# Where the 24 conditioning slabs of a two-layer diffusion trunk are loaded and multiplied: all ahead of layer 0, or 4 + 6 + 14

## What is computed

```
def trunk_layer(x, cvec, l, ...):
    mod = silu(cvec) @ w_mod[l] + b_mod[l]         # (6, 1024) per group: shift, scale, gate, shift, scale, gate
    h = rmsnorm(x, g[0]) * (1 + mod[1]) + mod[0]   # needs mod 0 and 1
    m = token_mixers(h)                            # 18 column panels of w_in, retention, attention, HGRN2, w_br, w_o
    x = x + mod[2] * rmsnorm(m, g[1])
    h = rmsnorm(x, g[2]) * (1 + mod[4]) + mod[3]
    f = swiglu(h) if l == 0 else moe(h)            # dense feed-forward in layer 0, top 2 of 8 experts in layer 1
    x = x + mod[5] * rmsnorm(f, g[3])
```

## Time and profile before

| | before |
|---|---|
| time, median of 3 runs (lowest, highest) | 1983.29 us (1982.0, 1985.23) |
| the profiled execution: its time | 1984.04 us |
| the profiled execution: span, first to last instruction | 1982.1 us |
| busy PE, DVE, ACT, POOL in the span | 88%, 63%, 50%, 6% |
| mean granted clock of TensorE | 0.936 of full speed |
| start of panel 0 of layer 0, from the span's start | 142.9 us |
| dense feed-forward on PE | 486 to 683 us |

### The profile page before, as it was taken

How to read it: one execution, slowest core, us unless ns; L and a number is a source line. 1 busy time by engine, 2 the same in 40 slices (tenths; PEclk the granted TensorE clock), 3 DMA queues, 4 the chain that set the end, 5 groups by cost and what they waited for, 6 DMA issues and landing times.

```text
span 1982.1 us, 21106 instructions
## 1 busy us (share of the span) xinstructions
PE 1750.0 (88%) x8190; PEld 1399.3 (71%) x8191; DVE 1257.7 (63%) x1081; ACT 988.9 (50%) x930; POOL 126.1 (6%) x78
## 2 busy tenths in 40 slices
PE   4569999976999779999875999989898989898996
PEld 1128888865788668888765777878787878787773
DVE  1115579843544365598643887878686868686872
ACT  3114353333444264543332767767676767675751
POOL 1001013200000010033100000000000000000000
PEclk9869999987999879999985999999999999998998
DMA  9994544414443424534232879798797979797850
GB/s 400 427 401 170 185 164 150 164 60 192 169 190 150 158 86 175 196 134 165 96 136 100 313 288 361 287 362 337 313 368 275 378 271 372 281 368 272 349 206 22
DMA packets 55795, 470.22 MB, mean 237 GB/s; under 512 B 6352, under 2 KB 6400, under 8 KB 8496
## 3 DMA queue, kind: packets, MB, share of 16 engines
q1 hardware_dynamic: 52848, 458.25, 59.8%
q0 software_dynamic: 2880, 11.02, 1.4%
HBM read 465.05 MB, written 4.19 MB: 237 GB/s over the span
## 4 chain that ended last, share of the span: by engine, by line
PE 83%; DMA 6%; ACT 4%; DVE 4%; issue 3%; POOL 0%; SPq 0%; POOLq 0%; ACTq 0%; DVEq 0%
PE ps L927 24%; PE ps L928 24%; PE ps L929 24%; DMA ring<-in_w_mod 5%; ACT w_hi L711 2%; PE ps L1097 2%; PE ps L989 1%; PE ps L1321 1%; PE ps L1059 1%; PE ps L901 1%; DVE ring_lo L1618 1%; PE ps L969 1%; PE ps L921 1%; DMA ring<-in_w_in 1%; ACT ring_lo L700 0%
## 5 line engine op out<-in xcount | busy, mean ns | idle before, releaser
L1618 DVE TENSOR_TENSOR ring_lo<-ring,w_hi 128x2048 fp32r<-128x2048 f32 x297 | 680.0, 2292 | 232.1 <-ACT w_hi L711 232.0
L927 PE MATMUL ps<-ring_lo,h_hi 128*128 128x512 f32 x1520 | 611.0, 402 | 31.0 <-issue 25.1
L711 ACT ACTIVATE w_hi<-ring 128x2048 fp32r<-128x2048 f32 x297 | 568.0, 1913 | 106.8 <-PE ps L929 97.3
L927 PEld LDWEIGHTS ps<-ring_lo,h_hi 128*128 128x128 f32 x1520 | 289.8, 191 | 93.9 <-issue 33.9
L929 PE MATMUL ps<-w_hi,h_hi 128*128 128x512 f32 x880 | 346.2, 393 | 0.0
L928 PE MATMUL ps<-w_hi,h_lo 128*128 128x512 f32 x880 | 346.1, 393 | 0.0
L1557 DVE TENSOR_TENSOR ring_lo<-ring,ring_lo 128x2048 fp32r<-128x2048 f32 x76 | 182.6, 2405 | 236.4 <-ACT ring_lo L700 235.7
L700 ACT ACTIVATE ring_lo<-ring 128x2048 fp32r<-128x2048 f32 x92 | 176.1, 1916 | 260.9 <-PE ps L929 215.4
L929 PE MATMUL ps<-ring_lo,h_hi 128*128 128x512 f32 x640 | 252.2, 394 | 0.0
L928 PE MATMUL ps<-ring_lo,h_lo 128*128 128x512 f32 x640 | 252.0, 394 | 0.0
L927 PE MATMUL ps<-ring_lo,act_hi 128*128 128x512 f32 x440 | 181.9, 413 | 41.6 <-DVE ring_lo L1618 41.6
(11 more groups left out here) (266 smaller groups left out, 1474.4 us busy)
## 6 DMA issues: line engine op xcount, KB each, us to landing
ring<-in_w_ff SPq DMA_DIRECT2D x297, 1024.0 KB, 6.9
ring<-in_w_in SPq DMA_DIRECT2D x36, 2048.0 KB, 8.1
ring<-in_w_mod SPq DMA_DIRECT2D x24, 2048.0 KB, 12.4
ring<-in_w_br SPq DMA_DIRECT2D x6, 2048.0 KB, 7.9
ring<-in_w_o SPq DMA_DIRECT2D x4, 2048.0 KB, 7.7
out<-state_out POOLq DMA_DIRECT2D x4, 512.0 KB, 4.5
x_sb<-in_x POOLq DMA_DIRECT2D x1, 1024.0 KB, 28.8
state<-in_s_ret POOLq DMA_DIRECT2D x2, 512.0 KB, 25.6
```

The costliest lines, as they stand in the source:

```text
L711: A(w_hi[p], ring[i % SLOTS][:, p * UNIT:(p + 1) * UNIT], ACT.Copy).then_inc(hi_ready[p], 1)
L927: mm(out, a_hi, b_lo, start=start, stop=False, skip_group_check=True)
L1618: V.tensor_tensor(ring_lo[i % SLOTS][:, part], ring[i % SLOTS][:, part], w_hi[p].bitcast(F32), ALU.subtract)\
```

## The change

It moves 20 of the 24 conditioning slabs. Slabs 0 to 3 stay in front. Slabs 4 and 5, 6 and 7, 8 and 9 are put into the list behind the panels 0, 1 and 2 of w_in, and PE multiplies them after `pieces` of these panels; group 1 is turned after panel 3, and panel 4 waits for DVE's reading of it. Two empty turns of the ring (`skip`) are put behind panels 5 and 10. With that, the ring deals out so: panels 0, 1, 2 and 3 of layer 0 all take slot 1, one after the other; panels 4 and 5 follow slabs 8 and 9; panel 6 takes the slot of 4, 7 that of 5, 8 that of 3, 9 that of 6, 10 that of 7, 11 that of 9, 12 that of 10, 13 that of 8. (Before, panel j takes the slot of panel j-3.) From the first projection on the slots are as before.

Slabs 10 to 23 go to two buffers `late` in the part of `u` that the mixer no longer needs. SP issues 10 and 11 behind the last load of w_o, after two more waits, and slab n+2 once PE is done with slab n, between the loads of the feed-forward. PE multiplies one slab in each slice i of the dense feed-forward (two in slices 3, 6 and 9), between the gate and up products of slice i and the down products of slice i-1. Both tiles' transposes share bank 6, and bank 7 accumulates the slabs.

```
@@ constants
-MOD_GROUPS = [range(0, MOD_SPLIT), range(MOD_SPLIT, 15), range(15, L * NSLAB_MOD)]
+MOD_GROUPS = [range(0, 4), range(4, 10), range(10, NMODS)]
+MOD_AFTER = {0: (4, 5), 1: (6, 7), 2: (8, 9)}
+MOD_FOLD_AFTER = 3
+SKIP_AFTER = (5, 10)
+MOD_IN_FFN = [[10 + i + sum(i > t for t in (3, 6, 9)) + n for n in range(2 if i in (3, 6, 9) else 1)] for i in range(NFS)]
-MOD_BANK = (0, 1, 2)
-MOD_TURN_BANK = (3, 0, 1)
+MOD_BANK = (0, 4, 7)
+MOD_TURN_BANK = (3, 1, 4)
@@ layer_slabs
-        slabs = [("mod", n // NSLAB_MOD, n % NSLAB_MOD) for n in range(L * NSLAB_MOD)]
+        slabs = [("mod", 0, n) for n in MOD_GROUPS[0]]
...
+        if l == 0:
+            slabs += [("mod", 0, n) for n in MOD_AFTER.get(j, ())] + [("skip", 0, j)] * (j in SKIP_AFTER)
@@ SP
+            def load_late(n):
+                q = n - MOD_GROUPS[2][0]
+                if q < 2:
+                    sp.wait_ge(hst_done, 1)
+                    sp.wait_ge(hsq_ready, 1)
+                else:
+                    sp.wait_ge(mod_done, n - 1)
+                sp.dma_start(late[q % 2], w_mod[n]).then_inc(late_in[q % 2], 16)
...
+                    for n in MOD_GROUPS[2][:2]:
+                        load_late(n)
                     for i in range(NFS):
+                        if i >= SLOTS:
+                            for n in MOD_IN_FFN[i - SLOTS]:
+                                load_late(n + 2)
                         load(("ffn", 0, i))
@@ ACT
                 if l == 0:
-                    copy_mod(1)
                     mix_split(0, 0)
-                    copy_mod(2)
...
+                    if l == 0 and j == MOD_FOLD_AFTER:
+                        copy_mod(1)
                     mix_split(l, 2 * c + 3)
...  (in ffn)
+                    if i == NFS - 1 and first:
+                        copy_mod(2)
@@ PE
-                    pe.wait_ge(mod_read, 1)
+                if l == 0 and j == MOD_FOLD_AFTER + 1:
+                    pe.wait_ge(mod_read, 2)
...  (in ffn)
-                              ins = nc.tensor.transpose(ps[:, 6 + t, j * P:(j + 1) * P],
+                              ins = nc.tensor.transpose(ps[:, 6, t * FS + j * P:t * FS + (j + 1) * P],
...
+                    if i < NFS and maps:
+                        for n in MOD_IN_FFN[i]:
+                            modulate(n)
+                    if i == NFS and maps:
+                        turn_mod(2)
...  (the order ahead of and in layer 0)
-            modulate(0)
+            for n in MOD_GROUPS[0]:
+                modulate(n)
             turn_rows(0, 0)
             turn_mod(0)
-            modulate(1)
-            turn_mod(1)
-            modulate(2)
-            turn_mod(2)
...
                     panel(l, j)
+                    if l == 0 and j == MOD_FOLD_AFTER:
+                        turn_mod(1)
                     pieces(l, j)
...
+                    if l == 0:
+                        for n in MOD_AFTER.get(j, ()):
+                            modulate(n)
@@ DVE
-                    read_mod(1)
-                    own(read_mod(2), mod_read, 1)
-                    modulation(0, 2, 6, mod_raw[:, 8 * MOD_FIRST:2 * NMOD], mod_rest, 1)
...  (behind ahead(l, "win", 3))
+                if l == 0:
+                    own(read_mod(1), mod_read, 2)
+                    modulation(0, 2, 5, mod_rest, 1)
...  (behind ffn(2, 0, True))
+                    own(read_mod(2), mod_read, 3)
+                    modulation(0, 5, 6, mod_rest, 2)
```

More of the change, by code:

```diff
@@ L178, in program @@
         e_out = u[:, 3 * D:11 * D]
+        late = [u[:, (3 + 4 * b) * D:(7 + 4 * b) * D] for b in range(2)]
         br_ = sb("br", 2 * D)
@@ L247, in program @@
         part_in = [[sem(f"part{p}_in{s}") for s in range(SLOTS)] for p in range(NPART)]
+        late_in = [sem(f"late_mod_in{b}") for b in range(2)]
         s_bias = sem("bias_loaded")
@@ L441, in load @@
                     sp.wait_ge(*released(before))
-                src = w_mod[key[1] * NSLAB_MOD + key[2]] if key[0] == "mod" else source[key[0]][key[1], key[2]]
+                src = w_mod[key[2]] if key[0] == "mod" else source[key[0]][key[1], key[2]]
                 sp.dma_start(ring[s][:, 0:src.shape[1]], src).then_inc(slab_in[s], 16)
@@ L457, in load_parts @@
                     sp.dma_start(ring[i % SLOTS][:, part], w_ff[n, i][:, part]).then_inc(part_in[p][i % SLOTS], 16)
-            for l in range(L):
[L460 to L470, removed]
+            def load_late(n):
[6 more added lines that the diff above has]
+                sp.dma_start(late[q % 2], w_mod[n]).then_inc(late_in[q % 2], 16)
+            for l in range(L):
+                for key in layer_slabs(l):
                     if key[0] != "skip":
@@ L473, in _ @@
                 if l == 0:
+                    for n in MOD_GROUPS[2][:2]:
+                        load_late(n)
                     for i in range(NFS):
+                        if i >= SLOTS:
+                            for n in MOD_IN_FFN[i - SLOTS]:
+                                load_late(n + 2)
                         load(("ffn", 0, i))
+                    for i in range(NFS - SLOTS, NFS):
+                        for n in MOD_IN_FFN[i]:
+                            if n + 2 < NMODS:
+                                load_late(n + 2)
             for s in range(SLOTS):
@@ L887, in _, with modulate @@
             mm = nc.tensor.matmul
-            def modulate(part):
+            def modulate(n):
+                part = [n in r for r in MOD_GROUPS].index(True)
                 slabs = MOD_GROUPS[part]
                 strips = P // STRIP
-                for i, n in enumerate(slabs):
-                    s, u, _ = plan[("mod", n // NSLAB_MOD, n % NSLAB_MOD)]
+                if part < 2:
+                    s, u, _ = plan[("mod", 0, n)]
                     pe.wait_ge(slab_in[s], 16 * (u + 1))
[L897 to L904, removed]
+                    w = ring[s][:, 0:KD * 512]
+                else:
+                    q = n - slabs[0]
+                    pe.wait_ge(late_in[q % 2], 16 * (q // 2 + 1))
+                    w = late[q % 2]
+                w = w.rearrange("p (k c) -> p k c", k=KD)
+                at = COND_PAD - 2 * (n - slabs[0])
+                for k in range(KD):
+                    to = STRIP * (k % strips)
+                    ins = mm(ps[to:to + STRIP, MOD_BANK[part], :], cond_pad[:, k, at:at + STRIP], w[:, k, :],
+                             start=(n == slabs[0] and k < strips), stop=(n == slabs[-1] and k >= KD - strips),
+                             skip_group_check=True)
+                ins.then_inc(mod_done, 1)
             def turn_mod(part):
@@ L1034, in gate_rows @@
             def gate_rows(l, n, m):
-                if l == 0 and n == 0:
-                    pe.wait_ge(mod_rest, 1)
+                if l == 0:
+                    pe.wait_ge(mod_rest, n + 1)
                 if n == 1:
@@ L1397, in read_mod, with modulation @@
                                      turned.rearrange("p c (n g) -> p n c g", g=2))
-            def modulation(l, first, end, raw, done, value):
+            def modulation(l, first, end, done, value):
                 blocks = slice(first * KD, end * KD)
+                raw = mod_raw[:, 2 * (NMOD * l + first * KD):2 * (NMOD * l + end * KD)]
                 link(V.tensor_tensor(modc.rearrange("p m k g -> p (m k) g")[:, blocks], raw.rearrange("p (n g) -> p n g", g=2),
@@ L1736, in _ @@
                 if l == 0:
-                    link(read_mod(0))
-                    modulation(0, 0, 2, mod_raw[:, 0:8 * MOD_FIRST], mod_ready, 1)
-                else:
-                    dve.wait_ge(mod_read, 1)
-                    modulation(1, 0, 6, mod_raw[:, 2 * NMOD:4 * NMOD], mod_ready, 2)
+                    own(read_mod(0), mod_read, 1)
+                    modulation(0, 0, 2, mod_ready, 1)
+                else:
+                    modulation(1, 0, 6, mod_ready, 2)
                 turn_read(l, 0)
```

19 lines of the change are left out of this document (7 added, 12 removed).

## The result

The changed kernel takes 2005.51 us (median of 4 runs, 2000.07 to 2011.42), the kernel before 1984.26 beside it: a ratio of 1.011, 95% interval 1.0093 to 1.0127. It is slower by 21 us (1.1%), where 16.5 was forecast (2000, with 1986 to 2010 as the range). The profiled execution has a span of 2003.3 us against 1982.1, 21.2 more.

What follows compares the result with a forecast made beforehand. DMA was taken to bound the stretch before panel 0, PE what follows. Terms -81.5 + 61.2 + 13.0 + 23.8 = +16.5 on the profiled span 1982.1 gave 1998.6, predicted as 2000 us, range 1986 to 2010.

Steps and rivals of the forecast that it cites:

- The front: Stretch before panel 0 of layer 0: panel 0 starts at 61.4 instead of 142.9, 81.5 us saved.
- Panels 0 to 3: Shared slot 1 makes gaps of 12.4, 19.1, 20.4 and 6.6, plus clock restarts: 61.2 us given back before panel 4.
- the 8.4 allowed: Panels 0 to 3: each restarts at the lower clock after a wait, 2.1 us each, 8.4 together.
- The fixed cost of a DMA: Lone 2 MB slab load: the skill page's 2.0 us fixed time gives 7.0 against the row's 8.1; sum then 1993.
- The short ring: Panels 4 to 12: some slabs lead by two panels, not three; stalls and clock add 13.0 us.
- the 8.8 up to level 0: After panel 11: time from the start of DVE's `forget(1)` to level 0's release, used for a 3.9 us stall.
- The dense feed-forward: 14 slabs at 1.8 us in its slices, less 1.41 covered by a wait: 23.8 us more; their loads fit.
- Hidden matmuls in the feed-forward: Rival: conditioning slabs cost PE nothing in the dense feed-forward; sum -7.3, 1976 us; chance 4%.
- A harmless short ring: Rival, panels 4 to 12: DVE and ACT have more room, the 13.0 falls away; +3.5, 1987 us; chance 10%.
- Late loads that collide: Rival, feed-forward: each of 14 late loads makes PE wait 2.5 us, with three clock restarts; 2010 us; chance 11%.
- A lone load in the time of its bytes: Rival, slab loads: 5.0 us to land, not 8.1; about 22 us less, 1978 us; chance 5%.
- A late front: Rival, before panel 0: x and the constants share DMA with slabs and land 8 us later; 2008 us; chance 5%.

Runs made afterwards that it cites:

- own-buffers run: Changed kernel with slabs 4 to 9 in two buffers of their own instead of the ring, empty turns right behind slab 3: 1947.52 us, ratio 0.9821.
- exchange run: Changed kernel with PE multiplying the two conditioning slabs behind panels 1 and 2 before the panel's turn, not after: 1999.24 us, ratio 1.0062.
- run without the late slabs: Changed kernel without loads, matmuls, copy and turn of its 14 feed-forward slabs, zeros written in their place: 1977.74 us, ratio 0.9967.
- run without loads: Changed kernel without the loads of slabs 12 to 23; their matmuls stay and read slabs 10 and 11 again: 2002.24 us, ratio 1.009.
- last version: own-buffers run with slabs 4 to 9 one panel earlier, and slabs 10 and 11 moved into the wait ahead of the feed-forward: 1934.78 us, ratio 0.9757.

## Why the prediction was right, by its own steps

The forecast was slower by 16.5, it is 21.2 in the profiled execution and 21.25 in the medians. The mechanism held: a front that is shorter by 81, most of it given back by the shared slot, and more than the rest by the short ring and the slabs in the feed-forward. The sum is 4.7 short, 2.8 of it in the feed-forward. In two stages the sum came out better than its parts, and that was luck. The steps, forecast against measured:

| step | forecast | measured |
|---|---|---|
| panel 0 starts | 61.4 | 62.2 |
| panel 0 to panel 4, beyond 49.4 | +61.2 | 111.2 - 49.4 = +61.8 |
| panel 4 to the end of panel 12 | +13.0 | (301.7 - 173.4) - (308.7 - 192.3) = +11.9 |
| from there to the feed-forward | 0 | +1.0 |
| dense feed-forward | +23.8 | 215.4 - 188.8 = +26.6 |
| rest | 0 | +0.7 |

**The front.** Right to 0.8: the chain behind x was untouched, and with four slabs it ends last.

**Panels 0 to 3.** Right, each stretch from one panel's start to the next within 1.2 us: 87.3 for panel 1 (forecast 86.8 by the terms), 122.7 for panel 2 and 156.5 for panel 3. There 121.0 and 154.4 follow from the terms, if the restart is put where the trace has it, on the turn and the slabs ahead of the panel. The own-buffers run shows the cause: without the shared slot all but the last of these waits vanish. The exchange run shows the second half of the argument, that slabs 6 to 9 stood behind the turn instead of under the load: 8.5 us of the 61.8. Here luck helped. The four restarts took about 2 more than the 8.4 allowed: panel 0 took 2.1 beyond 10.9, panel 1 took 3.2 (its first 14 matmuls at the lower clock), the turn and two slabs before panel 2 took 2.4 beyond their 4.7, those before panel 3 2.7. Against that, each lone load took 7.7 to 7.8 instead of 8.1, 1.0 less in all, and the step to panel 4 took 5.8 instead of 6.6.

**The fixed cost of a DMA.** The Trainium skill ("DMA: Bandwidth & Descriptors", "Anatomy of one DMA") gave an estimate of 7.0 for a lone 2 MB load; the chain has 7.80, 7.82 and 7.72 here, so this case does not agree. The section's figure is for loads issued by GpSimd, which the prediction did not say; these are issued by SP. The rows of before were nearer. The same page's rule to issue early and wait late ("Rules for kernel authors") is what the own-buffers run does, and there it is worth 58 us, the short ring's 9.5 among them.

**The short ring.** The sum was right to 1.1, but its terms were not, and that they cancel was luck. Waits of PE: 2.72 in panel 6 (forecast 3.2), 2.51 at the turn before panel 11 (1.0), 0.66 for level 0 (3.9) and 1.73 for unit 25 (none), together 7.6 against 8.1. Clock: I had 1.7 at panel 4, 1.5 in panel 6 and 1.7 at level 0. But the wait of 3.09 before panel 4 cost nothing (granted clock 1.00 from 173.4 to 182.0), nor did the two last ones (1.00 from 286.9 to 301.7). It fell in panel 6 and in panel 11, for 8 matmuls each: 2 x 8 x 0.2 = 3.2 against 4.9. Some 1.1 of the 11.9 I can't place.

PE was late at level 0 by the wait and the slow matmuls before it, so less was left of the 3.9. And unit 25 waited for something that the forecast had not as a term of its own, a DVE instruction that runs beside a split on POOL. Rows of the changed kernel, and behind the dots one of the run without the late slabs:

```profile
286.58 4.70 POOL L564 TENSOR_TENSOR ring_lo<-ring,ring_lo 128x2048 fp32r<-128x2048 f32 x1 [4.83 <-ACT ring_lo L714]
286.77 5.05 DVE L1557 TENSOR_TENSOR u<-u 128x512 f32<-128x512 f32 x1
...
283.09 4.87 DVE L1533 TENSOR_TENSOR u<-u 128x512 f32<-128x512 f32 x1
```

Instructions of DVE of this form take 0.69 otherwise. This one ends 0.5 us after POOL's split and is 4.4 longer, more than the 1.73 that PE then waits for unit 25. In the other run POOL's split stands at 282.79 to 287.41, so the long instruction is one that level 0 needs, and level 0 waits 7.54 instead of 0.66. The 4.86 of line 1498 in the earlier trace rows is of this kind too: POOL splits at 284.08 to 288.69 there, and the same four take 1.38 at 275.22. So the 8.8 up to level 0 in the forecast already had one such stretch in it.

**Between panel 12 and the feed-forward.** The 1.0 is one wait of PE, at line 999, that the kernel before doesn't have.

**The dense feed-forward.** The mechanism held, the price of a slab was the term that mattered most. I took 1.8, since I thought that the drain of its last matmul would overlap what follows. The trace shows no such gain. The timeline of slice 1 of the changed kernel:

```profile
506.89 0.39 PE L950 MATMUL ps<-w_hi,h_hi 128*128 128x512 f32 x1
507.21 1.92 PE L922 MATMUL ps<-u,cond_pad 128*32 128x512 f32 x16
509.07 0.50 PE L948 MATMUL ps<-ring_lo,act_hi 128*128 128x512 f32 x1
509.41 0.40 PE L949 MATMUL ps<-w_hi,act_lo 128*128 128x512 f32 x1
```

Between neighbours of the wide kind the start-to-start is 0.227. Around the slab it is 0.32 going in, 1.86 for the slab, and 0.34 for the first matmul behind it: 0.32 + 1.86 + 0.34 - 2 x 0.227 = 2.07 for each slab. The pitch of the slices says the same: 533.59 - 514.68 = 18.91 with one slab, against 534.99 - 518.18 = 16.81 before, 2.10. 13 slabs at 2.07 are 26.9, the first adds 15.78 - 15.33 = 0.45, and the last wait is 0.81 shorter for the turn of 1.1: 26.9 + 0.45 + 1.1 - 0.8 is 27.6, 1 above the 26.6 of the stage (double slabs in slices 3, 6 and 9 pay the edges once). The run without loads shows that 0.7 at most of it is DMA.

**The rivals.** Hidden matmuls in the feed-forward: out, 26.6 of them are paid. A harmless short ring: out, 9.5 alone. Late loads that collide: out, 0.7 at most. A lone load in the time of its bytes: out, 7.7 to 7.8. A late front: out.

What I left out was that the timed runs of the changed kernel spread over 11 us, the four of before over 4. Its mean granted clock in the four runs is 0.925 to 0.932. With more restarts there is more for the clock to vary in; that is only argued, though the exchange run shows one such case (14 and 13 slow matmuls where the changed kernel has none and 8).

## What to carry to other kernels

Work moved out of a stage that waits for DMA gains only if the next stage keeps its lead in loads: count for each consumer how many turns of work lie between the release of its slot and its use, and compare that with load plus preparation (7.8 + 4.2 = 12.0 us here against one panel of 10.9). An in-order queue spreads one late load to work that doesn't need it: here a turn of panel 0's columns waited for panel 2's slab. And fill the stretches in which the engine already waits (9.9 ahead of panel 0, 5.2 ahead of the feed-forward) before the ones where it is the bound; there a slab costs next to nothing (with two slabs ahead of it panel 0 started 0.4 later), in the slices 2.1.

## What the runs showed of the hardware

A block of 16 matmuls with weights of 32 columns, set between matmuls with 128, cost 2.07 us and not its own 1.86: the steps into and out of it take 0.1 each. A transfer of 2 MB that goes ahead of three of 1 MB in the same queue raised the median landing of these from 7.0 to 11.6 us. While POOL ran a split of 4.6 to 4.7 us, a DVE instruction that takes 0.69 otherwise took 4.87 to 5.05.

The length of a wait did not tell by itself whether PE's granted clock fell. It stayed up behind a wait of 1.64 us in the last version and behind 3.09 before panel 4 of the changed kernel (first matmul 0.47). It was down at once behind 2.78 before panel 4 of the own-buffers run (0.77), and behind 2.37 ahead of a projection in the kernel before: the first matmul there, at 417.02 us, took 0.80 and the next five 0.63 each, where 0.39 is usual. And behind 2.72 in panel 6 of the changed kernel it fell only 1.6 us after the restart. What decides between these is open.
